# A long convolution in a transformer kernel: its taps split into even and odd halves, two edits around it moved along

## The reference

```
def hyena_longconv(u, filt, bias):
    L = u.shape[1]
    n = 2 * L
    uf = jnp.fft.rfft(u.astype(jnp.float32), n=n, axis=1)
    kf = jnp.fft.rfft(filt, n=n, axis=0)
    y = jnp.fft.irfft(uf * kf[None], n=n, axis=1)[:, :L]
    return (y + u.astype(jnp.float32) * bias.astype(jnp.float32)).astype(u.dtype)

def hyena_mix(p, conv_w, conv_b, filt, bias):
    uc = dwconv3(p, conv_w, conv_b)
    x0, x1, v = jnp.split(uc, 3, axis=-1)
    return x0 * hyena_longconv(x1 * v, filt, bias)
```

## Time and profile before

| | us |
|---|---|
| median of 3 runs (2444.87 to 2445.99) | 2445.51 |
| the profiled execution's own time | 2445.26 |
| its span, first to last instruction | 2442.6 |
| TensorE busy | 2282.5 |
| VectorE busy | 1238.0 |
| ScalarE busy | 1052.4 |
| GpSimd busy | 645.7 |

### The profile page before, as it was taken

How to read it: one execution, slowest core, us unless ns; L and a number is a source line. 1 busy time by engine, 2 the same in 40 slices (tenths; PEclk the granted TensorE clock), 3 DMA queues, 4 the chain that set the end, 5 groups by cost and what they waited for, 6 DMA issues and landing times.

```text
span 2442.6 us, 31499 instructions
## 1 busy us (share of the span) xinstructions
PE 2282.5 (93%) x12106; PEld 1775.1 (73%) x12106; DVE 1238.0 (51%) x1917; ACT 1052.4 (43%) x1565; POOL 645.7 (26%) x286
## 2 busy tenths in 40 slices
PE   5998999889999999988999889999998999989997
PEld 2776656678888888866656558888886865778776
DVE  3665832253422334236676225525524249469998
ACT  3433831352322323225356135434433258458876
POOL 1220000322223222332300043444444420223233
PEclk8999999899999999988999989999999999999999
DMA  6421032113211231112411332233322322349997
GB/s 251 177 95 43 36 121 83 56 54 129 78 61 62 96 129 61 61 52 98 139 44 58 133 121 78 95 95 101 98 95 70 103 79 62 116 173 402 352 352 263
DMA packets 81181, 291.33 MB, mean 119 GB/s; under 512 B 10729, under 2 KB 13194, under 8 KB 80076
## 3 DMA queue, kind: packets, MB, share of 16 engines
q1 hardware_dynamic: 74192, 257.68, 30.5%
q10 hardware_dynamic: 3964, 17.95, 2.0%
q0 software_dynamic: 2880, 13.68, 1.4%
HBM read 283.50 MB, written 9.48 MB: 120 GB/s over the span
## 4 chain that ended last, share of the span: by engine, by line
PE 82%; DVE 9%; ACT 3%; issue 2%; POOL 1%; DMA 1%; DVEq 1%; SPq 0%; ACTq 0%
PE ps L673 40%; PE ps L720 12%; PE ps L696 4%; DVE mlo L2575 4%; PE ps L1374 3%; PE ps L1001 2%; PE ps L781 2%; PE ps L1017 2%; PE ps L954 2%; PE ps L1234 2%; PE ps L1392 2%; PE ps L1090 1%; PE ps L972 1%; POOL x L607 1%; PE ps L1069 1%
## 5 line engine op out<-in xcount | busy, mean ns | idle before, releaser
L601 POOL TENSOR_TENSOR wlo<-wraw,whi 128x1024 fp32r<-128x1024 f32 x208 | 502.2, 2416 | 1346.3 <-ACT whi L1415 705.9
L673 PE MATMUL ps<-hhi,whi 128*128 128x512 f32 x1624 | 592.3, 365 | 3.0 <-DVE hlo L2279 2.0
L673 PE MATMUL ps<-hlo,whi 128*128 128x512 f32 x1624 | 584.0, 360 | 0.0
L673 PE MATMUL ps<-hhi,wlo 128*128 128x512 f32 x1624 | 581.4, 358 | 0.0
L673 PEld LDWEIGHTS ps<-hhi,whi 128*128 128x128 f32 x1624 | 306.7, 189 | 83.4 <-issue 31.2
L673 PEld LDWEIGHTS ps<-hhi,wlo 128*128 128x128 f32 x1624 | 305.7, 188 | 47.9
L673 PEld LDWEIGHTS ps<-hlo,whi 128*128 128x128 f32 x1624 | 306.6, 189 | 45.6 <-issue 1.0
L2004 DVE SCALAR_TENSOR_TENSOR up<-ps,cconv,up 128x511 f32<-128x511 f32 (+1 forms) x132 | 83.2, 658 | 288.1 <-ACT up L1749 285.5
L2575 DVE TENSOR_TENSOR mlo<-mraw,mhi 128x1024 fp32r<-128x1024 f32 x147 | 205.3, 1426 | 5.6 <-ACT mhi L1863 5.5
L1422 ACT ACTIVATE whi<-wraw 128x1024 fp32r<-128x1024 f32 x132 | 138.9, 1052 | 145.9 <-PE ps L720 120.3
L1749 ACT ACTIVATE up<-ps,cconv 128x768 f32<-128x768 f32 (+1 forms) x88 | 77.8, 885 | 257.2 <-PE ps L673 256.7
(11 more groups left out here) (345 smaller groups left out, 3704.5 us busy)
## 6 DMA issues: line engine op xcount, KB each, us to landing
wraw<-in_w_all SPq DMA_DIRECT2D x288, 512.0 KB, 3.5
mraw<-in_w_moe SPq DMA_DIRECT2D x168, 512.0 KB, 6.3
mraw_b<-in_w_mod SPq DMA_DIRECT2D x10, 512.0 KB, 15.4
fl<-in_four ACTq DMA_DIRECT2D x2, 2048.0 KB, 8.1
hd<-in_hyf POOLq DMA_DIRECT2D x2, 2048.0 KB, 9.2
hi<-in_hyi ACTq DMA_DIRECT2D x2, 2048.0 KB, 9.4
slot_rows<-in_slot_rows ACTq DMA_DIRECT2D x1, 3612.0 KB, 20.2
xs<-slot_rows POOLq DMA_DIRECT2D x7, 516.0 KB, 7.4
```

The source lines that it names most:

```text
L601: pool.tensor_tensor(wlo[:, slot, :], wraw[:, AT_W[n] % RING, :], whi[:, slot, :].bitcast(F32), ALU.subtract).then_inc(lo_split, 1)
L673: m = pe.matmul(ps[:, bank + b, 0:w], a, r[:, c0:c0 + w], start=k == 0 and q == 0, stop=k == KT - 1 and q == 2)
```

## The change

1. The taps of filter and signal are ordered even ones first, odd ones after (`apart`, `folded`), and each half is transformed by itself, for only half of the frequencies. The sum of the two results is one frequency, the difference its mirror image. For 512 tokens a frequency tile now holds 256 frequencies in two result banks, so there are 2 such tiles, and 1 for the context. Each tile takes 8 forward matmuls of 256 columns for the filter and 8 for the signal (4 and 4 for the context). The way back is split in the same manner: 8 matmuls of 256 columns per channel half (4 of 128 for the context) (`folded_sums`, `folded_back`).
2. The additions are new work. ScalarE copies both filter banks into `hraw`, GpSimd forms sum and difference into `hsp` (it is in GpSimd's program behind the split of the third output slab), ScalarE copies the signal's odd bank, and VectorE now has nine operations per tile in place of five. The inverse table is fetched by GpSimd's queue ahead of the convolution, the context's tables by ScalarE's queue at its start.
3. Three quarters of the first output tiles, the 6 inner blocks that don't need the convolution, run inside it (`early_tile`): in the first block one tile before the way back and one after, in the second two before and one after. The last two inner blocks follow when the convolution's output is there (`early_tile_end`).
4. The modulation pairs move: 4 stay in the first block's convolution, none in the second's; the 4 at output tiles are at the first block's; 12 are in each half of the first block's feed-forward part, two tiles in three.
5. The rotations go to the banks of the last three input tiles, each waiting for its own bank (`rot_bank`); the last `mod_turn` of the input stage moves inside the last input tile.

```diff
-IN_PAIRS, HY_PAIRS, UP_PAIRS, OUT_PAIRS = (6, 8, 10, 12), 8, (2, 4, 6, 8, 10, 12), (0, 2, 4, 5)
-IN_G, HY_G, UP_G, OUT_G = (4, 16), (6, 18), 10, 22
+UP_GROUPS = 6
+IN_PAIRS, HY_PAIRS, OUT_PAIRS = (6, 8, 10, 12), 4, (0, 2, 4, 5)
+UP_PAIRS = tuple(2 + 3 * q + z for q in range(UP_GROUPS) for z in range(2))
+IN_G, HY_G, OUT_G, UP_G = (4, 22), 6, 8, 10
...
+    def rot_bank(L, j):
+
+        return bank2(L * LAYER_TILES + IN_T - 3 + j // 2) + j % 2
...
+                L = n // LAYER_SLABS
+                for f in range(3 if L == 0 else 2):
+                    t = fold_nth(L, 0) + f
+                    pool.wait_ge(sem("hraw_ready"), t + 1)
+                    pool.tensor_tensor(hsp[:, f, 0, :], hraw[:, f % 2, 0, :], hraw[:, f % 2, 1, :], ALU.add)
+                    pool.tensor_tensor(hsp[:, f, 1, :], hraw[:, f % 2, 0, :], hraw[:, f % 2, 1, :], ALU.subtract)\
+                        .then_inc(sem("hsp_ready"), 1)
...
+        def early_tile(n, t, bank, slot, rhs, width):
+
+            pe.wait_ge(acc_free, t - 2)
+            slab_ready(n)
+            for k in range(KT - 2):
+                hi, lo = rhs(k)
+                passes = [(wh(slot, k), hi), (wh(slot, k), lo), (wl(slot, k), hi)]
+                for c0, w, b in segs[width]:
+                    for q, (a, r) in enumerate(passes):
+                        pe.matmul(ps[:, bank + b, 0:w], a, r[:, c0:c0 + w], start=k == 0 and q == 0, stop=False)
+
+        def early_tile_end(bank, slot, rhs, width, ready, before):
+
+            for c0, w, b in segs[width]:
+                pe.wait_ge(ready, before + 2 * b + 2)
+                for k in (KT - 2, KT - 1):
+                    hi, lo = rhs(k)
+                    for q, (a, r) in enumerate([(wh(slot, k), hi), (wh(slot, k), lo), (wl(slot, k), hi)]):
+                        m = pe.matmul(ps[:, bank + b, 0:w], a, r[:, c0:c0 + w], start=False,
+                                      stop=k == KT - 1 and q == 2)
+            m.then_inc(slab_done, 1)
...
+            def last_turn(s, k):
+                if s == IN_T - 1 and k == 5:
+                    mod_turn(IN_G[L] + 1, 6)
...
-            mod_turn(IN_G[L] + 1, 6)
-
-            pe.wait_ge(acc_free, T0 + IN_T)
+
             for j in range(5):
+                pe.wait_ge(acc_free, T0 + IN_T - 2 + j // 2)
                 pe.wait_ge(sem("qn_ready"), 5 * L + j + 1)
-                pe.matmul(ps[:, j, :], rot[:, :], pxq[:, IN_DST[j], 0:TX], start=True, stop=True)\
+                pe.matmul(ps[:, rot_bank(L, j), :], rot[:, :], pxq[:, IN_DST[j], 0:TX], start=True, stop=True)\
...
-            for s, c0, nt_ in hsegs[L]:
...
-                for f in range(nt_):
-                    if f >= 2:
-                        pe.wait_ge(sem("hys_ready"), tile_nth(*K) + f - 1)
-                    for cs_ in range(2):
-                        for q in range(nt_):
-                            m = pe.matmul(ps[:, 4 + f % 2, cs_ * 256:cs_ * 256 + 256],
-                                          fwd[:, cs_, q, f * P:f * P + P], filt[:, q, cs_ * 256:cs_ * 256 + 256],
-                                          start=q == 0, stop=q == nt_ - 1)
-                    m.then_inc(sem("hk_ready"), 1)
...
-                            m = pe.matmul(ps[:, 6 + f % 2, cs_ * 256:cs_ * 256 + 256],
-                                          fwd[:, cs_, q, f * P:f * P + P], hut[:, c0 // P + q, :],
-                                          start=q == 0, stop=q == nt_ - 1)
-                    m.then_inc(sem("hu_ready"), 1)
...
-                pe.wait_ge(sem("hys_ready"), tile_nth(*K) + nt_)
-                pe.wait_ge(sem("hinv_in"), 16 * L + 32)
-                if s == 1:
-                    pe.wait_ge(sem("hyf"), 2 * seg_nth(L, 0) + 2)
+
...
+            def folded_sums(bank, table_, nq, f, rhs):
+
+                for cs_ in range(2):
+                    for par in range(2):
+                        for q in range(nq):
+                            m = pe.matmul(ps[:, bank + par, cs_ * 256:cs_ * 256 + 256],
+                                          table_[:, cs_, nq * par + q, f * P:f * P + P], rhs(nq * par + q, cs_),
+                                          start=q == 0, stop=q == nq - 1)
...
+            for f in range(2):
+                if f == 1:
+                    pe.wait_ge(sem("attn_out"), 2 * NQT * L + NQT * (2 if L == 0 else 1))
+                folded_sums(4 + 2 * f, hd5, 2, f, lambda q, c: hpm[:, q, c * 256:c * 256 + 256])\
+                    .then_inc(sem("hk_ready"), 1)
...
+            pe.wait_ge(sem("ut_ready"), T // P * L + ntt)
+            for f in range(2):
+                if f == 1:
+                    pe.wait_ge(sem("hraw_ready"), K0 + 2)
+                folded_sums(6 * f, hd5, 2, f, lambda q, c: hut[:, q, :]).then_inc(sem("hu_ready"), 1)
+                if two:
+                    hy_pair(2 + f)
+            if two:
+                pe.wait_ge(sem("hinv_in"), 32)
...
+                pe.wait_ge(sem("hraw_ready"), K0 + 3)
+            else:
+                pe.wait_ge(sem("hu_taken"), K0 + 1)
+            for s in range(EARLY_OUT[L][0]):
+                early_out(s)
+
+            def folded_back(bank, c, s, iv, half):
+
+                for par in range(2):
+                    nf = 2 - s
+                    for f in range(nf):
+                        for cs_ in range(2):
+                            m = pe.matmul(ps[:, bank, par * half:par * half + half],
+                                          hys[:, 2 * s + f, par, cs_ * 256 + c * P:cs_ * 256 + c * P + P],
+                                          iv[:, cs_, f, par * half:par * half + half],
+                                          start=f == 0 and cs_ == 0, stop=f == nf - 1 and cs_ == 1)
...
+            pe.wait_ge(sem("hys_ready"), K0 + 2)
+            for c in range(2):
+                folded_back(6 + c, c, 0, hi5, TX // 2)
+            if two:
+                pe.wait_ge(sem("hys_ready"), K0 + 3)
+                pe.wait_ge(sem("mod_taken"), HY_G + 2)
...
+            for s in range(EARLY_OUT[L][0], sum(EARLY_OUT[L])):
+                early_out(s)
             W = T if L == 0 else TX
             for s in range(OUT_T):
-                tile(S0 + IN_T + s, T0 + IN_T + s, bank2(T0 + IN_T + s), (S0 + IN_T + s) % RING, h_rhs, W)
-                if L and s in OUT_PAIRS:
+                if s < sum(EARLY_OUT[L]):
+                    early_tile_end(bank2(T0 + IN_T + s), (S0 + IN_T + s) % RING, h_rhs, W, sem("hy_out"), 4 * L)
+                else:
+                    tile(S0 + IN_T + s, T0 + IN_T + s, bank2(T0 + IN_T + s), (S0 + IN_T + s) % RING, h_rhs, W)
...
+                bank = (4, 6, 4)[f]
+                act.activation(hraw[:, f % 2, 0, :], ps[:, bank, :], ACT.Copy)
+                act.activation(hraw[:, f % 2, 1, :], ps[:, bank + 1, :], ACT.Copy).then_inc(sem("hraw_ready"), 1)
...
+                bias(HY_G + q, 3, mod_columns(HY_G + q))
+
+            K0 = fold_nth(L, 0)
+            if L == 0:
+                hy_bias(0)
+            for f in range(3 if L == 0 else 2):
+                dve.wait_ge(sem("hu_odd"), K0 + f + 1)
+                bank = (0, 6, 0)[f]
+                dve.tensor_tensor(huu[:, 0, :], ps[:, bank, :], hodd[f % 2][:, :], ALU.add)
+                dve.tensor_tensor(huu[:, 1, :], ps[:, bank, :], hodd[f % 2][:, :], ALU.subtract).then_inc(sem("hu_taken"), 1)
+                dve.wait_ge(sem("hsp_ready"), K0 + f + 1)
+                dve.drain()
+                dve.tensor_tensor(hb[:, :, :], hsp[:, f, :, :], huu[:, :, :], ALU.mult)
+                dve.tensor_tensor(ha[:, :, 0:256], hsp[:, f, :, 0:256], huu[:, :, 256:512], ALU.mult)
+                dve.tensor_tensor(ha[:, :, 256:512], hsp[:, f, :, 256:512], huu[:, :, 0:256], ALU.mult)
+                dve.drain()
+                dve.tensor_tensor(hyk[:, :, 0:256], hb[:, :, 0:256], hb[:, :, 256:512], ALU.subtract)
+                dve.tensor_tensor(hyk[:, :, 256:512], ha[:, :, 0:256], ha[:, :, 256:512], ALU.add)
+                dve.drain()
+                dve.tensor_tensor(hys[:, f, 0, :], hyk[:, 0, :], hyk[:, 1, :], ALU.add)
+                dve.tensor_tensor(hys[:, f, 1, :], hyk[:, 0, :], hyk[:, 1, :], ALU.subtract)\
+                   .then_inc(sem("hys_ready"), 1)
...
+                    dve.wait_ge(sem("hy_ready"), 2 * seg_nth(L, s) + c + 1)
+                    pairs = dst.rearrange("p (i two) -> p two i", two=2)
+                    dve.scalar_tensor_tensor(pairs, ps[:, (6, 2)[s] + c, 0:w].rearrange("p (two i) -> p two i", two=2),
+                                             rnorm[:, s, c:c + 1], pairs, ALU.mult, ALU.add)
```

245 lines of the change are left out of this document (114 added, 131 removed).

## The result

The changed kernel takes 2379.64 us (median of four runs, 2376.88 to 2381.46) against 2445.19 for the kernel before beside it: a ratio of 0.973, 95% interval 0.9715 to 0.9746, 65.6 us faster. The forecast was 2382. The profiled execution of the changed kernel took 2376.88, its span is 2375.0.

A forecast was written before the change was run, and what follows sets the result against it. TensorE, busy 93% of the span, was taken to bound the kernel. Terms 47.5 + 6.3 + 6.1 + 3.4 + 6.8 - 2.4 - 2.1 - 2.0 = 63.6 us gave 2382 us, range 2374 to 2392.

The forecast's parts named there:

- Fewer f32 matmuls: Convolutions of both blocks: folding saves TensorE matmul work, 26.4 us in the first and 21.1 in the second, together 47.5.
- First block, all of its terms: First block's convolution and output tiles: 26.4 us of matmuls saved and 6.3 of waits gone, less moved modulation work.
- Second block, the same stretch: Second block's convolution and output tiles: 21.1 us of matmuls, 6.1 of waits and 3.4 of half clock saved, less new waits.
- Waits that go: Convolutions: TensorE's waits for slabs, hys and hlo disappear, 6.3 us in the first block and 6.1 in the second.
- Half clock: Second block, behind the 3.61 us gap: TensorE's slow pair and 13 matmuls return to full pace, saving 3.4 us.
- the rotations' 6.8: Last input tile: bank waits of 3.04 and 2.04 us go, plus 1.7 for the second block's slower records; sum 6.8.
- the clock falls again: Rival: VectorE's chain sets the pace, with a longer gap before the way back and half clock; 2386 to 2393, chance 0.14.
- one of the signs by which the prediction said that it would be wrong: Second block's output tiles: the clock falling there would show the prediction wrong; no size given.
- New waits: Second block: TensorE waits 2.1 us for hys before the way back and 2 for wlo before the fourth output tile.
- the ratio 1.34: GpSimd's 128x1024 subtraction, 3.21 us beside VectorE against 2.39 alone, used to price contention in the first block at about 0.9.
- a spare of 2.3: First block before the way back: VectorE ends at 25.7, TensorE's early tile at 28.0, so no wait and 2.3 us spare.
- The rival of fetches that don't keep up: First block's feed-forward part: 24 pairs wait for slabs; 2447 and more at chance 0.02, 2393 to 2440 at 0.03.

The follow-up runs named there:

- b_mod: The kernel before with the modulation slabs placed as in the changed kernel, the old convolution kept; 2447.11 us, ratio 1.0011.
- a_noearly: The changed kernel with no output tile inside the convolution, the first one waiting for the whole convolution; 2404.63 us, ratio 0.9833.
- a_cont: The changed kernel with GpSimd's third (context) sum and difference held back until VectorE has finished its second frequency tile; 2379.21 us, ratio 0.9744.

## Why the prediction was right, step by step

- *Fewer f32 matmuls, 47.5.* Right: 20 + 20 + 16 + 8 matmuls in the first block, 16 + 16 + 16 in the second, at the paces forecast, 3.56 per group; the second block's 32 records even take 6.91 (1311.43 - 1304.52) where 7.12 was counted. The context's way back takes 1.8, estimated 1.9.
- *First block, all of its terms between attention's end and the feed-forward part.* My sum gives 26.4 + 6.3 - 0.8 (pairs and turns: 4.9 out, 5.7 in) = 31.9. Before, that stretch ran from the first transposes at 330.91 to 502.13, 171.2 us; after, from 326.74 to 465.24, 138.5: 32.7.
- *Second block, the same stretch.* My sum: 21.1 + 6.1 + 3.4 + 15.4 for 12 pairs and 6 turns that leave - 2.1 - 2.0 = 41.9. Before 1327.66 to 1467.09, after 1302.00 to 1398.86: 42.6.
- *Waits that go, 6.3 and 6.1.* The sizes hold, the reason was half of it. I put the slab waits down to slabs no longer fetched and took the `hys` and `hlo` waits as simply gone. b_mod shows that without the pairs these waits grow, and a_noearly that the changed kernel without early tiles has 10.0 us of them in the first block and 13.4 in the second. It is the early tiles that remove them, which my sum counted only as cover for the new chain. The forecast's number came out all the same because the change holds both edits.
- *Half clock, 3.4, and 1.7 of the rotations' 6.8.* Not a firm part of a sum. The changed kernel was profiled twice, and the waits are the same while the clock behind them is not. Here is the second execution; below the rows, from each execution, its slow stretch, with the granted clock as the third number from the end (second execution first):

```profile
1330.01 8.86 PE L1153 MATMUL ps<-hi,hys 128*128 128x256 f32 x32 [2.06 <-DVE hys L2354]
1349.01 0.47 PE L702 MATMUL ps<-hhi,whi 128*128 128x512 f32 x1 [1.94 <-POOL wlo L622]
```

```profile
1330.01:1338.52 8.51, 8.51 (x33) 7.20 (x33) 1.44 (x2) 0.63 (x1) 0.00 (x0) 0.80 0.00 0
```

```profile
1347.64:1350.62 2.98, 2.98 (x8) 2.32 (x7) 1.63 (x1) 0.00 (x0) 2.98 (x2) 0.50 0.63 199
```

  The way back takes 8.86 behind 2.06 where it took 7.17 behind 2.07; in the first execution seven output matmuls behind the 1.94 ran at 0.43 instead of 0.23, starting at 1347.64. Either way some 1.5 us that the sum had not. In a_cont, whose second block is the same, waits of 2.06 and 1.94 were followed by full clock both times. Of the rival "the clock falls again" that part came true, at less than half its price. It is also one of the signs by which the prediction said that it would be wrong: the clock did fall in the second block's output tiles, for seven matmuls of the first execution. The time stayed in the range because the cost is small and other places gained as much (last point). The Trainium skill (TensorE: Matmul & The Clock Gate, Loop structure matters more than you think) warns of idle stretches; these rows agree in kind and show that the same gap costs in one execution and not in the next.
- *New waits, 2.1 and 2.0.* Measured 2.07 and 1.94, by the mechanism given: VectorE's tile took 6.46 (6.4), the additions to values in PSUM with strided output 0.75 (the low bound of 0.7 held). That the numbers are so close is in part luck. The prediction's own terms give 24.3 - 22.4 = 1.9 and 4.5 - 2 x 1.37 = 1.8, not 2.1 and 2.0. On its scale TensorE was through with the forward groups at 13.6 (14.2), with the early tiles at 22.0 (22.4), and VectorE at 24.2 (24.3). Behind the first tile's end 0.2 us pass before ScalarE starts (1341.25 to 1341.45), which the count left out.
- *A wait that the sum never named.* 1.15 for `hut` in the second block: ScalarE waits there for VectorE's last `hlo` of attention before it copies. It takes nothing from the sum, since the kernel before has 0.4 for `hlo` and 0.3 and 0.6 for `hut` at the same place. Gone unnamed is a wait of 0.7 for a turn's `mrow` at the old convolution's end.
- *The term that was mis-sized: the contention in the first block.* By the ratio 1.34 I had 0.9 us of a spare of 2.3; it took 2.2, and `hys` was ready at 357.90, TensorE at 357.98. The Trainium skill (GPSIMD Engine Reference, 1. Specifications) named the mechanism rightly; a_cont agrees. The ratio was the wrong measure. It was GpSimd's slowdown and not VectorE's, the row behind it is a mean of 21 subtractions of 2.39 to 4.52 us, not of one that always has VectorE beside it, and by a_cont's rows the price is the rest of the other engine's instruction, about 1.1 us for each of the two additions. That nothing opened in the first block was luck by 0.1 us.
- *Not forecast:* 1.2 us in the norm behind the first feed-forward part, where 12 one-column sums take 1.36 (1060.59 - 1059.23) instead of 2.47, and 1.5 from the second block's Fourier mix to the end of its attention. In both places the waits are the same and the granted clock is not. In the norm it is 0.53 before and 1.00 after. In attention it is 0.61 before (1257.30 to 1265.00) and 0.78 after (1233.10 to 1241.00), behind the same wait of 2.35. Whether the change or the execution makes that difference isn't shown. These two are 2.7 of the 4.8 us by which the profiled execution's gain (68.4) exceeds the sum of 63.6. The rest is 0.8 up to the two Fourier mixes, 0.8 and 0.7 in the two stretches above, less 0.3 in the feed-forward part.

The rival of fetches that don't keep up is out: the 24 pairs of the feed-forward part wait for nothing, at a median of 3.5 us from issue to landing there.

## What to carry to other kernels

Halving the matmuls on the bounding engine frees their whole time only if something else fills the span in which the slower helpers still work: here the folding with the other edits gave 40 us, and another 25 came from putting independent output tiles into it. Before calling a filler worthless because it is moved to where it costs the same, ask what it covers: the modulation pairs taken out of the old convolution saved nothing. When new work is laid beside another engine's, take the price from rows of the engine that is on the path, and look at starts and ends and not at a mean: here it was a wait for the other's instruction to end, whatever the size of the own one.
